# Gates of the first tile placed in two halves, 64 tokens scattered packed by two, first gates loaded two keys later

## The reference

```
q = (xb @ wq).reshape(t, PEER_HEADS, 2, PEER_DQ // 2)
s = jnp.einsum('thpd,hpkd->thpk', q, subkeys)
s_top, i_top = lax.top_k(s, 16)                       # per token, head and side
cand = s_top[:, :, 0, :, None] + s_top[:, :, 1, None, :]
c_top, c_idx = lax.top_k(cand, 16)                    # of 256 candidates per head
e = i1 * N_KEYS + i2                                  # the expert of each of 8 x 16 slots
g = softmax(c_top)
act = gelu(einsum(u[e], xb));  out = einsum(g * act, v[e])
```

## Time and profile before

| | |
|---|---|
| median of 3 runs | 1958.81 us (1958.03 to 1958.87) |
| the profiled execution | 1960.15 us, its span 1958.8 us |
| TensorE matmul busy | 1944.7 us (99%), 9063 instructions |
| VectorE busy | 1206.2 us (62%) |
| ScalarE busy | 726.0 us (37%) |
| GpSimd busy | 922.8 us (47%) |
| 16 DMA engines | 375.49 MB, mean 192 GB/s |
| scatters at L1534 | 256 of 1701 ns mean |

### The profile page before, as it was taken

The page is one execution under the profiler, slowest core; times in us unless marked ns, Lnnn a source line. Parts: engine busy times, 40 slices in busy tenths (PEclk is TensorE's granted clock), DMA queues, the critical chain, the costliest instruction groups (busy, mean ns, idle before and its releaser), DMA issues.

```text
span 1958.8 us, 23646 instructions
## 1 busy us (share of the span) xinstructions
PE 1944.7 (99%) x9063; PEld 1591.0 (81%) x9063; DVE 1206.2 (62%) x2174; ACT 726.0 (37%) x1043; POOL 922.8 (47%) x639
## 2 busy tenths in 40 slices
PE   8999999999999999999999999999999999999999
PEld 6777888888888778888888888888888888777787
DVE  4464544599999662222223688888888874895344
ACT  3345543332333342222223333333333335635452
POOL 1000000007878888888871777776787500720000
DMA  7543433246666659666677899999999913231122
GB/s 260 193 140 125 149 124 108 65 145 140 151 145 145 137 118 274 145 146 146 146 167 263 278 382 372 376 350 377 350 376 360 389 63 98 86 97 54 52 89 86
DMA packets 183680, 375.49 MB, mean 192 GB/s; under 512 B 61840, under 2 KB 101264, under 8 KB 175120
## 3 DMA queue, kind: packets, MB, share of 16 engines
q1 hardware_dynamic: 109264, 277.03, 41.6%
q0 software_dynamic: 69088, 86.80, 17.1%
q10 hardware_dynamic: 5216, 10.16, 1.4%
HBM read 312.90 MB, written 60.97 MB: 191 GB/s over the span
## 4 chain that ended last, share of the span: by engine, by line
PE 96%; DVE 3%; ACT 1%; issue 1%; DMA 0%; ACTq 0%; DVEq 0%
PE bank L1702 36%; PE bank L329 18%; PE bank L331 18%; PE bank L330 18%; PE bank L2383 1%; PE bank L1251 1%; DVE x L1970 1%; PE bank L2363 1%; PE bank L573 1%; PE bank L1580 1%; DVE v_low L1959 1%; PE bank L2372 1%; PE bank L627 0%; PE bank L593 0%; PE bank L638 0%
## 5 line engine op out<-in xcount | busy, mean ns | idle before, releaser
L1534 POOL DMA_INDIRECT gates_scratch<-slot_gate,slot_place x256 | 435.5, 1701 | 243.5 <-DVE slot_place L1489 157.1
L1702 PE MATMUL bank<-xn_low,u_high 128*128 128x512 f32 x1024 | 403.1, 394 | 0.0
L1702 PE MATMUL bank<-xn_high,u_high 128*128 128x512 f32 x1024 | 398.8, 389 | 0.0
L1702 PE MATMUL bank<-xn_high,u_low 128*128 128x512 f32 x1024 | 398.6, 389 | 0.0
L1754 DVE TENSOR_TENSOR u_low<-u_raw,u_high 128x1024 fp32r<-128x1024 f32 x128 | 156.7, 1225 | 283.9 <-ACT u_high L1725 283.5
L329 PE MATMUL bank<-v_high,w_high 128*128 128x512 f32 x768 | 299.0, 389 | 0.3 <-DVE v_low L1959 0.3
L330 PE MATMUL bank<-v_low,w_high 128*128 128x512 f32 x768 | 298.8, 389 | 0.0
L331 PE MATMUL bank<-v_high,w_low 128*128 128x512 f32 x768 | 298.8, 389 | 0.0
L322 DVE TENSOR_TENSOR weights_low<-weights_raw,weights_high 128x1024 fp32r<-128x1024 f32 (+1 forms) x105 | 127.7, 1217 | 203.8 <-ACT weights_high L311 203.7
L1741 ACT ACTIVATE hidden<-bank 128x512 f32<-128x512 f32 x128 | 76.5, 598 | 419.6 <-PE bank L1702 415.6
L1702 PEld LDWEIGHTS bank<-xn_high,u_high 128*128 128x128 f32 x1024 | 192.3, 188 | 40.5
(11 more groups left out here) (352 smaller groups left out, 3066.8 us busy)
## 6 DMA issues: line engine op xcount, KB each, us to landing
u_raw<-in_peer_u SPq DMA_DIRECT2D x128, 512.0 KB, 4.0
v_raw<-in_peer_v SPq DMA_DIRECT2D x64, 1024.0 KB, 7.5
weights_raw<-in_w_in SPq DMA_DIRECT2D x62, 512.0 KB, 3.7
hidden_scratch<-hidden SPq DMA_DIRECT2D x128, 192.0 KB
hidden_in<-hidden_scratch SPq DMA_DIRECT2D x32, 768.0 KB, 11.8
gates_scratch<-nothing POOLq DMA_DIRECT2D x32, 576.0 KB, 3.0
gate_in<-gates_scratch SPq DMA_DIRECT2D x32, 576.0 KB, 8.5
weights_raw<-in_w_out SPq DMA_DIRECT2D x16, 512.0 KB, 3.7
```

Source lines behind the costliest of these rows:

```text
L1534: pool.engine.indirect_dma_start(gates, bass.IndirectOffsetOnAxis(p.slot_place[t][:, i:i + 1], 0), p.slot_gate[t][:, i:i + 1], None, compu ...
L1702: step = pe.engine.matmul(m.bank[b][:, :], left[:, k, :], right[:, k, :], start=(done == 0), stop=(done == 3 * KT - 1))
```

## The change

It does four things. PACKED goes from 32 to 64 tokens and PACKS from 4 to 2, so that 64 tokens of tile 2 are scattered by 64 DMAs, packed two slots abreast by 4 packing DMAs, and 64 tokens are built on TensorE in 4 blocks. The first tile's choosing is cut into two passes of four heads: each has 4 + 2 steps of searching and 3 of placing (gates with the match; product with sums; last sum with `place`), in place of 12 and 6. The first four heads can be scattered once they are placed (`gates_placed` 1). And the step that waits for the scatters and loads gates 0 moves from key 120 to key 122, behind the load of values 2; `gate_hidden(0)` moves from 123 to 124 and `split_gated(0)` from 124 to 125. Buffers of the table, the clearing and the stores follow from the constants.

```diff
-PACKED, PACKS = 32, 4
+PACKED, PACKS = 64, 2
...
-CHOICE_STEPS = HP // 2 + PEER_HEADS // 2
+CHOICES = [(0, 0, PEER_HEADS // 2), (0, PEER_HEADS // 2, PEER_HEADS)] + [(t, 0, PEER_HEADS) for t in range(1, TT)]
+PICKED_AFTER = (2, 4, 5, 6, 7)
+TURNED_CHOICES = PICKED_AFTER[BUILT + 1]
+
+
+def choice_steps(first, last):
+    return (last - first) + (last - first) // 2
+
+
+def placing_steps(first, last):
+    return 6 if last - first == PEER_HEADS else 3
...
-            if n == CHOICE_STEPS:
-                act.wait_ge(s.gate_shifted, t + 1)
-                act.engine.activation(p.picked[:, 2, :], p.picked[:, 2, :], ACT.Exp).then_inc(s.gate_powered, 1)
+    for nth, (t, first, last) in enumerate(CHOICES):
+        for n in range(choice_steps(first, last) + placing_steps(first, last)):
+            if n == choice_steps(first, last):
+                act.wait_ge(s.gate_shifted, nth + 1)
+                gate = p.picked[:, 2, first * PEER_TOPK:last * PEER_TOPK]
+                act.engine.activation(gate, gate, ACT.Exp).then_inc(s.gate_powered, 1)
...
+        size = heads * PEER_TOPK
+        if whole:
+            wide = [P, 2 * size, PEER_TOPK]
+            match = p.match[:, :, :, :].rearrange("p a k r -> p (a k) r")
+            chosen_rank = p.digit_value[:, :, :, :].rearrange("p a h k -> p (a h k)").unsqueeze(2).broadcast_to(wide)
+            matches = [(match, chosen_rank, p.picked[:, 0:2, :].rearrange("p a k -> p (a k)"))]
+        else:
+            wide = [P, size, PEER_TOPK]
+            matches = [(p.match[:, half, slots, :], p.digit_value[:, half, first:last, :].rearrange("p h k -> p (h k)").unsqueeze(2).broadcast_to(wide),
+                        p.picked[:, half, slots]) for half in range(2)]
+        for match, chosen_rank, both in matches:
+            dve.step(v.tensor_tensor(match, chosen_rank, p.ranks[:, :].unsqueeze(1).broadcast_to(wide), ALU.is_equal))
...
         n = PEER_TOPK // 2
         while n > 1:
-            dve.step(v.tensor_tensor(match[:, :, 0:n], match[:, :, 0:n], match[:, :, n:2 * n], ALU.add))
+            for match, chosen_rank, both in matches:
+                dve.step(v.tensor_tensor(match[:, :, 0:n], match[:, :, 0:n], match[:, :, n:2 * n], ALU.add))
...
     def add(t, head):
-        pool.wait_ge(s.gates_placed, t + 1)
+        pool.wait_ge(s.gates_placed, 2 + t if t or head >= PEER_HEADS // 2 else 1)
...
     def pack():
-        pool.wait_ge(s.gates_placed, BUILT + 1)
+        pool.wait_ge(s.gates_placed, 2 + BUILT)
...
     load_values(1)
     yield
+    yield
+    yield
+    load_values(2)
     for t in range(ADDED):
         sp.wait_ge(s.gates_added[t], 16 * HK)
     sp.wait_ge(s.gates_added[BUILT], 16 * HK // PACKS)
     load_gated(0)
-    yield
-    yield
-    load_values(2)
     yield
     load_gated(1)
...
     split_values(1)
     yield
+    yield
     split_gated(0)
-    yield
     yield
...
     split_values(1)
+    yield
     gate_hidden(0)
     yield
     split_gated(0)
-    yield
     yield
```

More of the change, by code:

```diff
@@ L1344, in choose_tensor @@
     yield
-    for t in range(TT):
-        for n in range(CHOICE_STEPS + 6):
+    for t, first, last in CHOICES:
+        for n in range(choice_steps(first, last) + placing_steps(first, last)):
             if t == BUILT + 1 and n == 3:
                 b = GATE_BANKS[0]
-                pe.wait_ge(s.picked, t)
+                pe.wait_ge(s.picked, TURNED_CHOICES)
                 m.await_bank(b)
@@ L1395, in choose_vector @@
     yield
-    for t in range(TT):
+    for nth, (t, first, last) in enumerate(CHOICES):
         tile = tile_of(t)
-        for hp in range(0, HP, 2):
+        heads, whole = last - first, last - first == PEER_HEADS
+        slots = slice(first * PEER_TOPK, last * PEER_TOPK)
+        for hp in range(2 * first, 2 * last, 2):
             top_sixteen(dve, [(p.scores[:, tile, hp + i, :], p.work[i][:, 0:N_KEYS], p.top[:, hp + i, :], p.places[:, hp + i, :])
@@ L1402, in choose_vector @@
         dve.settle()
-        dve.step(v.tensor_copy(p.keys[:, :, :, :].rearrange("p h a r -> p (h a) r"), p.places[:, :, :]))
-        for h in range(0, PEER_HEADS, 2):
+        dve.step(v.tensor_copy(p.keys[:, first:last, :, :].rearrange("p h a r -> p (h a) r"), p.places[:, 2 * first:2 * last, :]))
+        for h in range(first, last, 2):
             for i in range(2):
@@ L1411, in choose_vector @@
             yield
-        gate = p.picked[:, 2, :].rearrange("p (h k) -> p h k", h=PEER_HEADS)
-        wide = [P, PEER_HEADS, PEER_TOPK]
+        gate = p.picked[:, 2, slots].rearrange("p (h k) -> p h k", h=heads)
+        wide = [P, heads, PEER_TOPK]
         dve.settle()
@@ L1434, in choose_vector @@
             dve.settle()
-        chosen_rank = p.digit_value[:, :, :, :].rearrange("p a h k -> p (a h k)").unsqueeze(2).broadcast_to(wide)
-        dve.step(v.tensor_tensor(match, chosen_rank, p.ranks[:, :].unsqueeze(1).broadcast_to(wide), ALU.is_equal))
+        size = heads * PEER_TOPK
+        if whole:
+            wide = [P, 2 * size, PEER_TOPK]
[8 more added lines that the diff above has]
+            dve.step(v.tensor_tensor(match, chosen_rank, p.ranks[:, :].unsqueeze(1).broadcast_to(wide), ALU.is_equal))
         dve.settle()
@@ L1439, in choose_vector @@
         for half in range(2):
-            part = p.match[:, half, :, :].rearrange("p (h k) r -> p h k r", h=PEER_HEADS)
-            of_rank = p.keys[:, :, half, :].unsqueeze(2).broadcast_to([P, PEER_HEADS, PEER_TOPK, PEER_TOPK])
+            part = p.match[:, half, slots, :].rearrange("p (h k) r -> p h k r", h=heads)
+            of_rank = p.keys[:, first:last, half, :].unsqueeze(2).broadcast_to([P, heads, PEER_TOPK, PEER_TOPK])
             dve.step(v.tensor_tensor(part, part, of_rank, ALU.mult))
         dve.settle()
-        yield
+        if whole:
+            yield
         n = PEER_TOPK // 2
         while n > 1:
-            dve.step(v.tensor_tensor(match[:, :, 0:n], match[:, :, 0:n], match[:, :, n:2 * n], ALU.add))
+            for match, chosen_rank, both in matches:
+                dve.step(v.tensor_tensor(match[:, :, 0:n], match[:, :, 0:n], match[:, :, n:2 * n], ALU.add))
             dve.settle()
@@ L1451, in choose_vector, with place @@
         yield
-        both = p.picked[:, 0:2, :].rearrange("p a k -> p (a k)")
-        v.tensor_tensor(both, match[:, :, 0], match[:, :, 1], ALU.add).then_inc(s.picked, 1)
+        for match, chosen_rank, both in matches:
+            v.tensor_tensor(both, match[:, :, 0], match[:, :, 1], ALU.add).then_inc(s.picked, 1)
+        if whole:
+            yield
+        place(m, keep, p, t, nth, slots)
         yield
-        place(m, keep, p, t)
-        yield
-def place(m, keep, p, t):
+def place(m, keep, p, t, nth, slots):
     dve, s = m.dve, m.s
     v = dve.engine
[L1464 to L1467, removed]
+    key1, key2, gate = (p.picked[:, i, slots] for i in range(3))
+    dve.wait_ge(s.picked, PICKED_AFTER[nth])
+    first, both = (tile[:, slots] for tile in p.place_value)
+    if nth == 0:
         dve.step(v.tensor_tensor(p.place_square[:, :], keep.ident[:, :], keep.counting[:, :], ALU.mult))
@@ L1473, in place @@
             dve.step(v.tensor_scalar(p.token[:, i:i + 1], p.token[:, 0:1], float(i * P), None, ALU.add))
-    dve.step(v.tensor_copy(p.slot_gate[t][:, :], gate))
+    dve.step(v.tensor_copy(p.slot_gate[t][:, slots], gate))
     dve.settle()
@@ L1488, in place @@
     else:
-        v.tensor_copy(p.slot_place[t][:, :], both).then_inc(s.gates_placed, 1)
-        dve.wait_ge(s.gates_placed, t + 1)
+        v.tensor_copy(p.slot_place[t][:, slots], both).then_inc(s.gates_placed, 1)
+        dve.wait_ge(s.gates_placed, nth + 1)
 def row_by_dram(m, n, scale, row, relaid):
```

19 lines of the change are left out of this document (9 added, 10 removed).

## The result

The changed kernel takes 1975.11 us in the median of its runs (1974.98 to 1976.33); the kernel before, run beside it on the same chip, 1958.42. The ratio is 1.0086 [1.0072, 1.0099]: slower, by 16.7 us, where I forecast 11.8.

A forecast was written before the change was run, and what follows sets the result against it. TensorE was taken to bound the kernel, with VectorE nearly full beside it. Terms -4.3 + 1.2 + 12.9 + 2.0 = +11.8 us on 1958.8 gave 1970.6 us; range 1956 to 1977.

The forecast's parts named there:

- case A: The forecast itself: key 127 on TensorE waits for the gates; 1962 to 1978 us by the bounds, chance 0.77.
- Fewer gate matmuls: TensorE, hidden stage: 16 of 48 pairs of gate matmuls go, at 0.270 us each; -4.3 us.
- Early lag: First tile placed in halves: VectorE is late with u_low at key 24 and TensorE waits; +1.2 us, bounds 0 to 3.
- Scatter's start: GpSimd's first scatter starts 31.3 us earlier, at 411.5 us, since the first half is placed sooner.
- Scatter's end: GpSimd's last scatter is out at 1063.8 us instead of 1036.4, +27.4 us, allowed 4 us either way.
- packing's gap: GpSimd's time for packing DMAs: 4 of 8 go, -2.6 us on the scatter chain.
- Clearing and landing waits stay: GpSimd's waits for clearing and for scatters to land stay unchanged, though heads of eight replace heads of four.
- Release: SyncE's wait for all scatters ends 4.3 us after GpSimd's last scatter, at 1068.1 us.
- Landing of hidden_in: The first gates' hidden_in lands 9 us after going out, at 1078.3 us; bounds -1.7 to +6.
- The load of u_raw: Key 127's load, queued on SyncE behind the wait for scatters, ends about when the gates' data does; no added time.
- TensorE stands 12.9: Before key 127, wanted at 1068.4 us, TensorE waits for u_low until 1081.3; +12.9 us.
- Restart: After the pause TensorE runs key 127 at a slower clock; +2 us, at least none and up to 3.

The follow-up runs named there:

- The slower pace: The changed kernel with VectorE's choosing spread over more keys (4 steps in 3 keys instead of 3 in 2, from key 7 to 55): 1968.38 us, 1.0049.
- the scatter in time: The changed kernel without the scatters of the last two heads of tile 1 (32 of 320), their gates left out of the result: 1956.42 us, 0.9989.

## Why the prediction was right, and where its sizes were off

The sign, the place and the mechanism were right: case A. The time was 1975.1 where I said 1970.6, inside the range. Step by step:

- **Fewer gate matmuls, -4.3:** right. 64 in place of 96, and TensorE's place moves by 4.3 us between key 25 and key 66.
- **Early lag, +1.2:** right in kind, 1.6 in size. The half's matches took 2.36, the products 1.29, the six sums 1.86 and the last sums 0.46, where I had 2.40, 1.3, 1.85 and 0.5. u_low of key 24 ended at 499.1, 2.0 later than in the kernel before, where I had 1.6, and TensorE lost 1.3 there against my 1.2. The other 0.3 it lost at key 14, for which I had nothing. The slower pace removes both.
- **Scatter's start, 411.5:** 411.61.
- **Scatter's end, 1063.8:** this is the step that failed, in its size. It was 1069.8, outside the 4 us I had allowed. From the start of the first scatter to the end of the last it took 658.2 us instead of 593.6: 64.5 more, where I had 58.7. In parts:
  - the 32 more scatters: 59.1, where I had 60.3;
  - time beyond 1.54 us in the scatters: 3.2 more before 640 us (I had 3.6), 2.4 less between 640 and 1000 us (I had 2.6), and 3.5 more after 1000 us, for which I had nothing. Late scatters now lie beside VectorE's first splits for the combine stage; two of them, the one of 3.37 us in the fence above and one of 2.56, make up 2.9 of it;
  - packing's gap: 1.9 less, where I had 2.6;
  - the two landing waits of the packed heads: 9.2 (6.43 and 2.79, see the fence above) against 6.2, so 3.0 more. "Clearing and landing waits stay" was wrong for these two; those before 640 us did stay.

  Before, GpSimd's timeline had:

```profile
1018.10 1.54 POOL L1550 DMA_INDIRECT gates_scratch<-packed_gate,packed_place  x1 [2.08 <-DMA gates_scratch<-packed_gate,packed_place]
...
1029.32 1.54 POOL L1550 DMA_INDIRECT gates_scratch<-packed_gate,packed_place  x1 [4.14 <-DMA gates_scratch<-packed_gate,packed_place]
```

- **Release, 4.3 after the scatter's end:** 1.7, and 1.5 to 1.7 in all six kernels in which SyncE waited. In the kernel before SyncE had come late to a wait that was already over, so rows 6 gave an upper bound and I used it as the value. The two errors partly cancel: release at 1071.5 against 1068.1.
- **Landing of hidden_in:** 8.3 us from issue; I took 9.
- **The load of u_raw, which "ends at about the same time and changes nothing":** wrong by 1.3 us. In the burst it took 9.8 us to land and was the later of the two. Taking it out of the burst returned only 0.6 at TensorE, since hidden_in then came later. That points to the burst as a whole, some 400 GB/s, rather than to one load in it; no run takes the burst apart further.
- **TensorE stands 12.9:** 16.2. u_low ended 3.7 later than I had it (1085.0 against 1081.3), and TensorE came 0.5 later.
- **Restart, +2:** 2.7. Key 127 took 1093.21 - 1085.05 = 8.16 us instead of 5.44. The row I had (transposes at the start at 421 ns, with a granted clock of 1.00) pointed the right way without showing the clock; here the records show it, 0.50 from 1075 on and for the first 12 matmuls. By the Trainium skill, TensorE: Matmul & The Clock Gate, in its part on the clock gate, an idle array falls to 1.2 GHz and gets 2.4 GHz back only once it has worked: the trace agrees, and without that rule the sum would have been lower by the 2 that I took, and so further off.

Sum as measured: -4.3 + 1.6 + 16.2 + 2.7 = +16.2, the difference of the spans. Of the 4.4 us between that and the forecast, 3.3 are the wait, 0.7 the restart and 0.4 the lag.

The experiments bear the mechanism out from three sides: with the scatter in time the loss is gone (1956.4); with a later or earlier release the time follows it, with 903.5, 903.7, 903.8 and 904.0 us between release and end in the four kernels whose VectorE takes the gates ahead of key 127's u_low, with releases between 1063.8 and 1091.2; and with u_low taken out of the chain the pause moves to w_low. This is also why the 4.3 us don't show at all: whatever TensorE gains before the wait only makes it wait longer. In the run with key 127's load moved TensorE came to its wait 2.2 us sooner than in the changed kernel (its hidden stage had begun 2.1 sooner in that profile), and the end stayed.

## What to carry over

When work moves from a bound engine to a chain on another engine, find the wait in which that chain ends and work out its end against the moment at which somebody first comes to it; past that point each microsecond of the chain costs a whole one, and what was saved on the bound engine is lost with it. Look what stands behind such a wait in its queue and ahead of the urgent instruction on the engine that consumes the data, and move both, but count the time of the transfers that the release sets off together. A size that just fits (48 tokens here, in place of 32 or 64) is worth trying before an order that hides the excess.

## What the runs showed of the hardware

- **A restart costs 2.4 to 3.0 us, whether the pause is 9 us or 39.** TensorE's first 12 matmuls after the pause came at 0.427 us instead of 0.227, at a granted clock of 0.50 (the first took longer still, 0.59), and that cost 2.7 us after a pause of 16.2. Over six kernels it was 2.7, 2.4, 2.5, 2.7, 3.0 and 3.0 us after pauses of 9.0, 11.3, 13.6, 16.2, 17.8 and 39.4 us, with 11 to 14 slow matmuls.
- **A scatter waits for a long two-input instruction of VectorE.** The scatter of 4.97 us at 494.31 and the one of 3.37 us at 1044.48 (fence above) lie beside these instructions:

```profile
493.45 4.42 DVE L1459 TENSOR_TENSOR match<-digit_value,ranks 128x4096 f16<-128x4096 f16 x1
...
1044.14 2.29 DVE L1985 TENSOR_TENSOR v_low<-v_raw,v_high 128x2048 fp32r<-128x2048 f32 x1 [5.07 <-ACT v_high L1932]
```

  Both ended 1.4 us after the instruction. Over all eleven kernels 43 scatters began inside a match of this size or a v_low; 42 of them ended 1.41 to 1.43 us after it, whenever they had begun, and one 1.54 after it. By the Trainium skill, SBUF — State Buffer, in its part on who interferes with whom, a VectorE instruction with two SBUF inputs and a GpSimd instruction that reads SBUF exclude each other for a whole instruction. The trace agrees in the size of the stop; no run here shows which port it is.
- **The landing of scatters isn't constant.** The first of the two waits for a packed head to land was 6.43, 7.73, 6.15, 1.81, 2.61 and 5.59 us in six kernels with the same 64 packed scatters (the changed kernel, then the runs in the order above). It goes with what SyncE has just issued. In the changed kernel the wait of 6.43 began at 1028.04, and SyncE's queue had:

```profile
1026.85 0.45 SPq L1823 DMA_DIRECT2D v_raw<-in_peer_v  x1
```

  Of the 24 such waits after 900 us in the eleven kernels, the five that began 1.1 to 1.6 us after a load of v_raw (1 MB) were 5.6 to 7.7 us long; the four that began 2.4 to 2.9 us after one, 2.8 to 4.3; the five that began 1.0 to 1.5 us after a load of u_raw alone (512 KB), 2.8 to 4.1; the other ten, 1.7 to 2.9. No run moves only such a load, so this is a pattern and not a cause shown. A chain whose heads wait for one another should be given some 5 us where its waits can fall behind such loads.
